# Sums of exponentials inverted in eight pieces per head inside attention, and loaded broadcast in the last projection

## The chip, the cores and the metric

The kernel runs on one NeuronCore of one Trainium2 chip. The metric is device time in microseconds (us), the median of several executions. An engine is one of TensorE (PE; its weight loads are shown as PEld), VectorE (DVE), ScalarE (ACT), GpSimd (POOL) and the engine that here only issues transfers, SyncE (SP). Each runs its own list of instructions in order and waits on semaphores for the others.

## The reference

One step of a two-layer decoder trunk over a prompt of 2048 rows and 8 sample rows, model width 1024. Layer 0 mixes a gated MLP and a linear recurrence. Layer 1 is an attention with a forget gate, 16 heads of 64 columns:

```
s = q @ k * scale + cq - ck            # cumulative log-forget bias, causal mask
p = softmax(s);  att = p @ v
y = x + (att * silu(g)) @ w_out1       # w_out1 is 1024 x 1024
```

The kernel doesn't divide by the sum of the exponentials inside the attention. It computes `exp(s - max) @ v`, gates it with silu(g), and stores it unnormalised to DRAM as `att` (1024 x 2056), beside the sums `lsum` (16 heads x 2056 columns; the 8 sample columns hold 1.0, since those rows are normalised at once). The last stage divides.

## The kernel before

The stages run one after another with a barrier between them: norm and layer 0, output projection 0, projection 1 together with the sample rows' scores, `past` (decay of the cached rows), `attention` (lines 1708 to 2260) and `out1` (2263 to 2431).

**attention.** A unit u is one head h = u // 4 and one quarter c = u % 4 of the prompt (512 query columns). It has 4(c+1) steps, one per block of 128 keys, so a head has 40 steps and the whole stage N = 640. `schedule()` (1741) writes out one list, SEQ, which every engine walks in the same order, doing its part of each entry. The entries:

- QK (step n): PE multiplies keys by queries into one of two PSUM buffers, ACT takes the exponential (2165), POOL adds it into the unit's `acc` (2037).
- M: the maximum pass, 22 steps ahead of QK. PE multiplies into MX, a ring of two PSUM buffers (2072), DVE reduces each to a maximum (2200). `ring_free` (2048) makes PE wait, before it writes a ring buffer, until the content two entries earlier has been read. There is one M at nearly every step, behind that step's QK. PE walks its list in order, so a late maximum also holds up every QK and PV behind it.
- PV: values by exponentials, for four steps at a time (2113). OE and OF finish a unit: ACT copies, DVE adds the halves (2214, 2215) and gates (2218), SP stores.
- LS (once per head): PE sums `acc` over its partitions into a ring buffer (2121), ACT copies it to `lt` (2177), SP stores one row of each 32 to `lsum` (1918). `lt` is [128, 512]: four quarters of the head, each replicated over 32 partitions.
- SD ... VC: the sample rows' attention, one batch row per 80 steps, so its small steps SD to SR fall on steps 1 to 10 of every second head only.

If E is the first step of a new head, the old head's last PV comes at E+1, its OF at E+5 and its LS at E+6. Below, "M9" stands for the maximum entry at step E+9. A boundary is called odd where E = 40, 120, ..., 600 (8 of them) and even where E = 80, 160, ..., 560 (7 of them); the sample rows' small steps are beside the even ones. The sixteenth LS stands at the very end of the list.

**out1.** 17 tiles, 16 of 128 rows and one of 8. Per tile: SP loads `att` (512 KB, 1024 pieces of 512 B) three tiles ahead (2291) and `x` (2295); DVE inverts 128 columns of the sums (2358); PE spreads the 16 inverted rows over 128 partitions with a 0/1 matrix `expand`, `turn_out` (2403 to 2410: 8 fp32 matmuls, 16 as the trace counts them); DVE multiplies (2365); ACT and DVE split the result into a high and a low part (2341, 2372); PE does `product` (2412), 48 matmuls of 512 columns recorded at lines 112 to 114; DVE adds x (2378); SP stores. `turn_out` of tile n+1 stands ahead of `product` of tile n. At the start of the stage 16 weight loads of 256 KB, ACT's high parts (2351) and DVE's low parts (2392) run beside the first product.

Of the kernel before, what the change touches and what calls it, by code (L numbers as in the profile page):

```python
# [33 lines left out]
P = 128  # L34
# [1673 lines left out]
def attention(nc, z, a, C, D, out):  # L1708
# [27 lines left out]

    def first_odd(u):

        return 0 if u % NC else P

    def schedule():
# [50 lines left out]
        for u in range(U):  # L1792
            for kb in range(blocks(u)):
                seq += loads.pop(n, [])
                for v in turn_at.pop(n, []):
                    turn(v)
                for w in later.pop(n, []):
                    if w[0] == "LS":
                        sums(w[1])
                    else:  # L1800
                        seq.append(w)
                seq.append(("QK", u, kb, n))
                for _ in range(min(2, min(len(todo), n + 1 + LEAD) - done)):
                    v = maximum()
                    if v is not None:
                        turn_at.setdefault(n + 3, []).append(v)
                if kb % G == G - 1:
                    pending.append((u, kb - G + 1, n - G + 1))
                if pending and pending[0][2] + G - 1 <= n - 2:
                    p = pending.pop(0)  # L1810
                    weigh(p)
                    if p[1] == blocks(p[0]) - G:
                        later.setdefault(n + 4, []).append(("OF", p[0]))
                        if p[0] % NC == NC - 1:
                            later.setdefault(n + 5, []).append(("LS", p[0] // NC))
                seq += side.pop(n, [])
                n += 1
# [5 lines left out]
        sums(H - 1)  # L1823
        assert n == N and done == len(todo) and not turn_at and not loads and not side
# [5 lines left out]
    with ExitStack() as ctx:  # L1830
# [53 lines left out]
        lst = S.sem("sums_stored")  # L1884
# [4 lines left out]
        def _(sp):  # L1889
# [26 lines left out]
            def store_sums(h):  # L1916
                sp.wait_ge(lsd, h + 1)
# [38 lines left out]
            for w in SEQ:  # L1956
# [4 lines left out]
                elif w[0] in ("OF", "LS"):  # L1961
                    due.append([2, *w])
# [7 lines left out]
                elif w[0] == "QK":  # L1970
                    for d in due:
                        d[0] -= 1
                    while due and due[0][0] <= 0:
                        d = due.pop(0)
                        if d[1] == "LS":
# [5 lines left out]
            for d in due:  # L1981
                if d[1] == "LS":
# [205 lines left out]
        def _(dve):  # L2188
# [6 lines left out]
            for w in SEQ:  # L2195
# [11 lines left out]
                elif w[0] == "OF":  # L2207
# [10 lines left out]
                    nc.vector.tensor_tensor(og[u % 2][:], og[u % 2][:], SG[u % 2][:], ALU.mult).then_inc(oadd, 1)  # L2218
                elif w[0] == "SD":
# [43 lines left out]
def out1(nc, z, a, C, D, out):  # L2263


    TILES = [(n, P, n * P) for n in range(z.NT)] + [(z.NT, z.B, z.T)]
    N = len(TILES)
    HALF = z.D // 512
    with ExitStack() as ctx:
# [7 lines left out]
        ls, rl = S.sb("ls", [z.H, z.TS]), S.sb("rl", [z.H, z.TS])  # L2277
        expand = S.sb("expand", [z.H, z.D])
        pp = S.ps("pp", [P, 2, z.D])
        rb = S.ps("rb", [P, 2, z.KB, P])  # L2280
        (l_in, w_hi, w_lo, exd, recd, spread, divided, m_hi, m_lo, prd, added) = S.sems(
            "lsum_in weight_hi weight_lo expanded lsum_inverted spread divided mixed_hi mixed_lo product added")
# [5 lines left out]
        def _(sp):  # L2288
            def load_mixed(n, rows, col):
                if n >= 3:  # L2290
                    sp.wait_ge(divided, n - 2)
                sp.dma_start(mt[:, n % 3, :, 0:rows],
                             D.att[:, ds(col, rows)].rearrange("(k p) t -> p k t", p=P)).then_inc(m_in[n % 3], 16)

# [10 lines left out]
            sp.dma_start(ls[:], D.lsum).then_inc(l_in, 16)  # L2305
# [18 lines left out]

        @block.gpsimd
        def _(pool):
            nc.gpsimd.memset(expand[:], 1.0).then_inc(exd, 1)
            pool.wait_ge(exd, 1)
            nc.gpsimd.affine_select(out=expand[:], in_=expand[:], compare_op=ALU.is_ge, fill=0.0, base=0,
                                    pattern=[[1, z.D]], channel_multiplier=-z.HD).then_inc(exd, 1)  # L2330
            pool.wait_ge(exd, 2)
            nc.gpsimd.affine_select(out=expand[:], in_=expand[:], compare_op=ALU.is_ge, fill=0.0, base=z.HD - 1,
                                    pattern=[[-1, z.D]], channel_multiplier=z.HD).then_inc(exd, 1)
# [22 lines left out]
        def _(dve):  # L2356
            def invert(n, rows, col):
                nc.vector.reciprocal(rl[:, ds(col, rows)], ls[:, ds(col, rows)]).then_inc(recd, 1)  # L2358

            def divide(n, rows):  # L2360
                dve.wait_ge(spread, n + 1)
# [3 lines left out]
                nc.vector.tensor_tensor(md[:, n % 2, :, 0:rows], mt[:, n % 3, :, 0:rows], rb[:, n % 2, :, 0:rows],  # L2365
# [14 lines left out]
            dve.wait_ge(l_in, 16)  # L2380
            invert(*TILES[0])
            invert(*TILES[1])
# [10 lines left out]
            for n, rows, col in TILES:  # L2393
                if n + 2 < N:
                    invert(*TILES[n + 2])
# [6 lines left out]
        def _(pe):  # L2402
            def turn_out(n, rows, col):
                pe.wait_ge(recd, n + 1)
                if n >= 2:
                    pe.wait_ge(divided, n - 1)
                for k in range(z.KB):
                    last = nc.tensor.matmul(rb[:, n % 2, k, 0:rows], expand[:, k * P:(k + 1) * P], rl[:, ds(col, rows)],  # L2408
                                            start=True, stop=True)
                last.then_inc(spread, 1)  # L2410

# [13 lines left out]

            pe.wait_ge(exd, 3)
            turn_out(*TILES[0])
            for n, rows, col in TILES:
                if n + 1 < N:
                    turn_out(*TILES[n + 1])  # L2430
                product(n, rows)
# [92 lines left out]
```

## Time and profile before

| what | us |
|---|---|
| median of 3 runs | 3041.19 (3039.72 to 3047.91) |
| the profiled execution's own time | 3042.56 |
| its span, first to last instruction | 3040.8 |
| attention, about | 1798 to 2797 of the span |
| out1, about | 2802 to 3041 of the span |
| the chain that ended last, by line (the page) | the product's lines 112, 113 and 114 2% of the span each, the spread's line 2408 1%, all others 0% |
| PE / DVE / ACT / POOL busy, share of the span | 92% / 52% / 34% / 45% |

Start times are counted in us from the first instruction. In a timeline row the first number is the start, the second how long the group lasted, and "x" how many instructions it holds; a group in square brackets is idle time of the engine before it and what ended it. The granted clock is 1.00 at TensorE's full 2.4 GHz and 0.50 at 1.2 GHz. An instruction's recorded duration runs from its start to its end; consecutive ones overlap a little, so four reductions of 0.69 us take 2.54 us together.

### The profile page before, as it was taken

How to read it: one execution, taken by the hardware profiler on the slowest of the kernel's cores; microseconds unless marked ns; L12 is line 12 of the kernel's file. 1: busy time of each engine (PE TensorE's matmuls, PEld its weight loads, DVE VectorE, ACT ScalarE, POOL GpSimd, SP SyncE). 2: the span in 40 equal slices, each digit the busy share in tenths (PEclk: the TensorE clock that was granted, in tenths of full speed). 3: DMA queues.
4: the chain of work that ended last, by engine and by line, in shares of the span. 5: the costliest groups of instructions: out<-in, count | busy, mean ns of one | idle time of the engine just before them, and what ended most of it. 6: DMA issues, size and time to landing. Idle time of an engine off the chain costs nothing. (4 is left out here: it accounts for less than half of the span.)

```text
span 3040.8 us, 46331 instructions
## 1 busy us (share of the span) xinstructions
PE 2789.8 (92%) x17133; PEld 2224.5 (73%) x17133; DVE 1592.0 (52%) x2154; ACT 1026.1 (34%) x1725; POOL 1377.5 (45%) x986
## 2 busy tenths in 40 slices
PE   3899999869989999999999739999999999998999
PEld 3899999757749989999899725555555555554887
DVE  4244333343545789865555465555645555453432
ACT  4333325312452222221122104454444455444100
POOL 0000000010003885469999836777776777776000
PEclk9999999979999999999999959999999999999999
DMA  4101111055635888788888767787897877874531
GB/s 122 44 28 47 46 35 37 14 182 173 183 119 170 293 288 276 252 276 272 268 261 275 220 152 221 207 242 217 218 252 205 240 211 221 238 212 140 168 119 63
DMA packets 327914, 547.68 MB, mean 180 GB/s; under 512 B 76093, under 2 KB 220129, under 8 KB 319212
## 3 DMA queue, kind: packets, MB, share of 16 engines
q1 hardware_dynamic: 246604, 454.31, 50.7%
q10 hardware_dynamic: 78080, 75.65, 7.6%
q0 software_dynamic: 3008, 14.81, 1.3%
q8 instruction: 135, 2.21, 0.3%
q14 instruction: 87, 0.71, 0.1%
HBM read 449.58 MB, written 95.12 MB: 179 GB/s over the span
## 5 line engine op out<-in xcount | busy, mean ns | idle before, releaser
L1174 POOL TENSOR_TENSOR p_kq<-p_kq 128x1024 f32<-128x1024 f32 x256 | 624.4, 2465 | 373.9 <-DMA p_kq<-in_cache_k_dram 373.5
L2037 POOL TENSOR_TENSOR at_acc<-at_acc,at_w 128x512 f32<-128x512 f32 (+3 forms) x576 | 645.2, 1120 | 229.5 <-ACT at_w L2165 165.7
L112 PE MATMUL p_pb<-p_w,x_xh 128*128 128x256 f32 x2048 | 593.0, 290 | 15.6 <-DVE p_w L1505 15.6
L2200 DVE TENSOR_REDUCE at_mx<-at_mx 128x1 f32<-128x512 f32 (+3 forms) x640 | 382.7, 608 | 427.2 <-PE at_mx L2072 311.9
L113 PE MATMUL p_pb<-p_w,x_xh 128*128 128x256 f32 x2048 | 580.3, 283 | 0.0
L114 PE MATMUL p_pb<-p_w,x_xl 128*128 128x256 f32 x2048 | 579.9, 283 | 0.0
L2165 ACT ACTIVATE at_w<-at_st,c_nckt 128x512 f32<-128x512 f32 (+3 forms) x640 | 389.6, 623 | 366.1 <-PE at_st L2098 193.2
L1607 DVE TENSOR_REDUCE p_sc<-p_kq 128x16 f32<-128x1024 f32 x256 | 310.0, 1216 | 201.6 <-POOL p_kq L1174 201.4
L112 PEld LDWEIGHTS p_pb<-p_w,x_xh 128*128 128x128 f32 x2048 | 391.2, 191 | 28.2 <-DVE p_w L1505 17.4
L113 PEld LDWEIGHTS p_pb<-p_w,x_xh 128*128 128x128 f32 x2048 | 392.9, 192 | 0.0
L114 PEld LDWEIGHTS p_pb<-p_w,x_xl 128*128 128x128 f32 x2048 | 392.1, 191 | 0.0
L112 PE MATMUL l_pb<-x_xh,l_wh 128*128 128x412 f32 x800 | 290.8, 364 | 7.4 <-DVE l_wl L875 7.4
L2113 PE MATMUL at_o<-at_w,at_v 128*64 128x512 f32 (+3 forms) x1280 | 282.7, 542 | 0.5 <-ACT at_w L2165 0.5
L114 PE MATMUL l_pb<-x_xh,l_wl 128*128 128x412 f32 x800 | 280.4, 350 | 0.0
L113 PE MATMUL l_pb<-x_xl,l_wh 128*128 128x412 f32 x800 | 280.2, 350 | 0.0
L2072 PE MATMUL at_mx<-at_km,at_q 128*128 128x512 f32 (+3 forms) x640 | 250.2, 393 | 28.8 <-POOL at_onesh L2012 21.6
L2096 PE MATMUL at_st<-at_q,at_k 128*128 128x512 f32 (+3 forms) x640 | 263.9, 412 | 0.8 <-ACT at_w L2165 0.8
L112 PE MATMUL o_pp<-o_wh,o_mh 128*128 128x512 f32 (+1 forms) x544 | 221.3, 407 | 35.1 <-DVE o_wl L586 22.2
L2098 PE MATMUL at_st<-at_q,at_k 128*128 128x512 f32 (+3 forms) x640 | 235.2, 367 | 0.0
L2096 PEld LDWEIGHTS at_st<-at_q,at_k 128*128 128x128 f32 x640 | 121.2, 189 | 135.9 <-issue 111.2
L113 PE MATMUL o_pp<-o_wl,o_mh 128*128 128x512 f32 (+1 forms) x544 | 216.7, 398 | 0.0
L114 PE MATMUL o_pp<-o_wh,o_ml 128*128 128x512 f32 (+1 forms) x544 | 216.2, 397 | 0.0
(296 smaller groups left out, 3802.9 us busy)
## 6 DMA issues: line engine op xcount, KB each, us to landing
p_kq<-in_cache_k_dram SPq DMA_DIRECT2D x256, 512.0 KB, 4.7
at_vp<-in_cache_v_dram SPq DMA_DIRECT2D x256, 512.0 KB, 5.2
o_mt<-mixed SPq DMA_DIRECT2D x32, 512.0 KB, 4.9
p_raw<-in_w_in_dram ACTq DMA_DIRECT2D x32, 512.0 KB, 5.8
at_q<-qh SPq DMA_DIRECT2D x32, 512.0 KB, 10.5
at_k<-kh SPq DMA_DIRECT2D x32, 512.0 KB, 8.2
l_raw<-in_w_in_dram SPq DMA_DIRECT2D x20, 512.0 KB
mixed<-l_w POOLq DMA_DIRECT2D x8, 1028.0 KB, 4.2
```

Of the source, the lines that this page charges most:

```text
L112: nc.tensor.matmul(out, lhs[0], rhs[0], start=(k == 0), stop=False)
L113: nc.tensor.matmul(out, lhs[0], rhs[1], start=False, stop=False)
L114: return nc.tensor.matmul(out, lhs[1], rhs[0], start=False, stop=(k == nk - 1))
L1174: nc.gpsimd.tensor_tensor(kq[:, slot[page]], kq[:, slot[page]], kq[:, slot[query]], ALU.mult).then_inc(kmul, 1)
L1607: nc.vector.tensor_reduce(sc[:, b % 2].rearrange("p (h g) -> p h g", g=z.PG)[:, :, r], by_head(kq[:, slot["p", g]], z.H), AX.X, ALU.add).t ...
L2037: nc.gpsimd.tensor_tensor(t[:, 512 - wd:512], t[:, 512 - wd:512], W[n % RW][:, 0:wd], ALU.add).then_inc(accd, 1)
L2072: last = nc.tensor.matmul(MX[r % 2][:, 0:wd], Q2[s][:, t * P:(t + 1) * P], KM[s][:, seg * 512:seg * 512 + wd], start=True, stop=seg < c)
L2096: nc.tensor.matmul(ST[n % 2][:, 0:wd], K1[s][:, ks], Q1[s][:, q0:q0 + wd], start=True, stop=False)
L2098: last = nc.tensor.matmul(ST[n % 2][:, 0:wd], K2[s][:, ks], Q2[s][:, q0:q0 + wd], start=False, stop=not diagonal)
L2113: last = nc.tensor.matmul(O[u % 2][y:y + HD, 512 - wd:512], V[s][:, kb + x, :], W[(n + x) % RW][:, 0:wd], start=kb + x < 2, stop=kb + x >= ...
L2165: nc.scalar.activation(W[n % RW][:, 0:wd], ST[n % 2][:, 0:wd], ACT.Exp, bias=C.nckt[:, kb, u // NC:u // NC + 1]).then_inc(ex, 1)
L2200: nc.vector.reduce_max(mx[:, u % 2, j, seg:seg + 1], MX[r % 2][:, 0:wd], AX.X).then_inc(mread, 1)
```

## The change

Two parts that need each other. In attention, DVE inverts `lt` in place before it is stored, in DC = 8 pieces of 64 columns per head, one at the head of each of the steps E+7 to E+14 (an entry "OI"); the last head's eight pieces stand at the end of the list. Piece 0 waits for ACT's copy of the sums. SP's store of the head's row waits for the eighth piece. `lsum` in DRAM then holds inverted sums.

In out1, the load of the sums, DVE's inversions, POOL's build of `expand` and all of PE's `turn_out` go. In their place SP issues, directly behind each load of an `att` tile, two DMAs that read the tile's 8 even and 8 odd head rows from DRAM and write each to 64 partitions, into `rb` in SBUF (three buffers). DVE's multiply waits for them instead of for PE, and reads both inputs from SBUF.

```
+    DC = 8
...
                         if p[0] % NC == NC - 1:
                             later.setdefault(n + 5, []).append(("LS", p[0] // NC))
+                            for x in range(DC):
+                                later.setdefault(n + 6 + x, []).append(("OI", x, p[0] // NC))
...
         sums(H - 1)
+        for x in range(DC):
+            seq.append(("OI", x, H - 1))
...
             def store_sums(h):
-                sp.wait_ge(lsd, h + 1)
+                sp.wait_ge(linv, DC * (h + 1))
...
-                elif w[0] in ("OF", "LS"):
-                    due.append([2, *w])
+                elif w[0] == "OF" or w[0] == "OI" and w[1] == DC - 1:
+                    due.append([2, w[0], w[-1]])
...
+                elif w[0] == "OI":
+                    _, x, h = w
+                    cols = slice(512 // DC * x, 512 // DC * (x + 1))
+                    if x == 0:
+                        dve.wait_ge(lsd, h + 1)
+                    nc.vector.reciprocal(lt[:, cols], lt[:, cols]).then_inc(linv, 1)
...
+                for x in range(2):
+                    sp.dma_start(rb[x * z.HD:(x + 1) * z.HD, n % 3, :, 0:rows],
+                                 D.lsum[:, ds(col, rows)].rearrange("(k x) t -> x k t", x=2)[x].partition_broadcast(z.HD)).then_inc(r_in[n % 3], 16)
...
-            sp.dma_start(ls[:], D.lsum).then_inc(l_in, 16)
...
-                dve.wait_ge(spread, n + 1)
+                dve.wait_ge(r_in[n % 3], 32 * (n // 3 + 1))
...
-                nc.vector.tensor_tensor(md[:, n % 2, :, 0:rows], mt[:, n % 3, :, 0:rows], rb[:, n % 2, :, 0:rows],
+                nc.vector.tensor_tensor(md[:, n % 2, :, 0:rows], mt[:, n % 3, :, 0:rows], rb[:, n % 3, :, 0:rows],
...
-                for k in range(z.KB):
-                    last = nc.tensor.matmul(rb[:, n % 2, k, 0:rows], expand[:, k * P:(k + 1) * P], rl[:, ds(col, rows)],
-                                            start=True, stop=True)
...
-            pe.wait_ge(exd, 3)
-            turn_out(*TILES[0])
             for n, rows, col in TILES:
-                if n + 1 < N:
-                    turn_out(*TILES[n + 1])
                 product(n, rows)
```

## Rows read from the trace of the kernel before

**Rows 1.** The chain that ended last, in order of time, in out1: start, us, what.

```profile
2801.76 3.21 DMA o_ls<-lsum
...
2806.08 3.76 PE o_rb L2408 x16
...
2867.25 1.98 PE o_rb L2408 x16
...
2880.33 1.98 PE o_rb L2408 x16
```

**Rows 2.** Windows: length; busy (count) of PE, PEld, DVE, ACT, POOL; clock, DMA share, GB/s.

```profile
1798.00:2797.00 999.00, 966.54 (x5320) 553.87 (x5320) 537.33 (x947) 482.04 (x793) 717.63 (x664) 0.99 0.78 218
1951.13:1958.00 6.87, 5.75 (x31) 3.55 (x29) 6.76 (x14) 3.25 (x6) 5.35 (x6) 1.00 0.51 115
2806.00:2814.60 8.60, 7.16 (x32) 6.90 (x32) 5.04 (x7) 4.73 (x8) 0.00 (x0) 0.50 1.07 364
2814.60:2819.40 4.80, 4.79 (x11) 3.81 (x12) 4.80 (x9) 3.61 (x8) 0.00 (x0) 0.50 1.05 390
2869.00:2882.10 13.10, 13.10 (x67) 10.81 (x65) 4.45 (x5) 1.06 (x1) 0.00 (x0) 1.00 0.39 121
3013.97:3017.38 3.41, 3.41 (x10) 2.67 (x9) 0.00 (x0) 0.00 (x0) 0.00 (x0) 0.50 0.17 67
```

**Rows 3.** Timeline of PE at the start of one tile of out1.

```profile
2866.86 0.39 PE L114 MATMUL o_pp<-o_wh,o_ml 128*128 128x512 f32 x1
2867.18 2.05 PE L2408 MATMUL o_rb<-o_rl,o_expand 16*128 16x128 f32 x16
2869.16 0.50 PE L112 MATMUL o_pp<-o_wh,o_mh 128*128 128x512 f32 x1
```

**Rows 4.** Groups by line and shape, DVE's reciprocals: busy us, mean ns, idle before.

```profile
L2358 DVE RECIPROCAL o_rl<-o_ls 16x128 f32<-16x128 f32 x16 | 14.8, 930 | 7.9 <-DMA o_ls<-lsum 7.9
...
L903 DVE RECIPROCAL l_ss<-l_ss 128x16 f32<-128x16 f32 x4 | 1.0, 254 | 21.5 <-ACT l_ss L839 21.5
```

**Rows 5.** Timeline at the first odd boundary (E = 40): ACT, DVE and PE.

```profile
1888.41 0.60 ACT L2177 ACTIVATE at_lt<-at_mx 128x512 f32<-128x512 f32 x1 [2.24 <-PE at_mx L2121]
...
1889.27 1.39 DVE L2200 TENSOR_REDUCE at_mx<-at_mx 128x1 f32<-128x512 f32 x2 [3.47 <-PE at_mx L2072]
...
1890.89 0.69 DVE L2200 TENSOR_REDUCE at_mx<-at_mx 128x1 f32<-128x512 f32 x1 [0.23 <-PE at_mx L2072]
...
1892.98 0.41 DVE L2200 TENSOR_REDUCE at_mx<-at_mx 128x1 f32<-128x256 f32 x1
...
1894.17 2.54 DVE L2200 TENSOR_REDUCE at_mx<-at_mx 128x1 f32<-128x512 f32 x4 [0.78 <-PE at_mx L2072]
...
1895.01 0.40 PE L2072 MATMUL at_mx<-at_km,at_q 128*128 128x512 f32 x1
...
1895.71 0.34 PE L2072 MATMUL at_mx<-at_km,at_q 128*128 128x384 f32 x1
...
1900.33 2.20 DVE L2200 TENSOR_REDUCE at_mx<-at_mx 128x1 f32<-128x512 f32 x3 [3.63 <-PE at_mx L2072]
```

**Rows 6.** Timeline at the first even boundary (E = 80): DVE and PE.

```profile
1951.13 1.28 DVE L2200 TENSOR_REDUCE at_mx<-at_mx 128x1 f32<-128x512 f32 x2
...
1957.38 1.83 DVE L2200 TENSOR_REDUCE at_mx<-at_mx 128x1 f32<-128x512 f32 x3
...
1958.15 0.40 PE L2072 MATMUL at_mx<-at_km,at_q 128*128 128x384 f32 x1
```

**Rows 7.** Timeline at the end of attention: DVE and SP.

```profile
2796.24 0.68 DVE L2218 TENSOR_TENSOR at_og<-at_og,at_sg 64x512 f32<-64x512 f32 x1
...
2797.51 0.52 SPq L1918 DMA_DIRECT2D lsum<-at_lt  x1
```

**Rows 8.** DMA issues: out<-in, engine, count, KB each, median us to landing.

```profile
o_mt<-att SPq DMA_DIRECT2D x16, 512.0 KB, 4.8
...
o_gb<-in_norm_g_dram SPq DMA_DIRECT2D x1, 512.0 KB, 8.3
```

More of the change, by code:

```diff
@@ L1883, in attention @@
         ogst = S.sems("out_stored0 out_stored1")
-        lst = S.sem("sums_stored")
+        lst, linv = S.sem("sums_stored"), S.sem("sums_inverted")
         v_in = S.sems("pages_in0 pages_in1")
@@ L1974, in _ @@
                         d = due.pop(0)
-                        if d[1] == "LS":
+                        if d[1] == "OI":
                             store_sums(d[2])
@@ L1981, in _ @@
             for d in due:
-                if d[1] == "LS":
+                if d[1] == "OI":
                     store_sums(d[2])
@@ L2276, in out1 @@
         xt = S.sb("x", [P, 3, z.D])
-        ls, rl = S.sb("ls", [z.H, z.TS]), S.sb("rl", [z.H, z.TS])
-        expand = S.sb("expand", [z.H, z.D])
+        rb = S.sb("rb", [P, 3, z.KB, P])
         pp = S.ps("pp", [P, 2, z.D])
-        rb = S.ps("rb", [P, 2, z.KB, P])
-        (l_in, w_hi, w_lo, exd, recd, spread, divided, m_hi, m_lo, prd, added) = S.sems(
-            "lsum_in weight_hi weight_lo expanded lsum_inverted spread divided mixed_hi mixed_lo product added")
+        (w_hi, w_lo, divided, m_hi, m_lo, prd, added) = S.sems(
+            "weight_hi weight_lo divided mixed_hi mixed_lo product added")
+        r_in = S.sems("rsum_in0 rsum_in1 rsum_in2")
         w_in = [S.sem(f"weight_in{m}") for m in range(HALF * z.KB)]
@@ L2323, in _ @@
                 sp.wait_ge(y_st[s], 16 * len(range(s, N, 3)))
[L2325 to L2333, printed above, removed]
         @block.scalar
@@ L2356, in _ @@
         def _(dve):
-            def invert(n, rows, col):
-                nc.vector.reciprocal(rl[:, ds(col, rows)], ls[:, ds(col, rows)]).then_inc(recd, 1)
             def divide(n, rows):
-                dve.wait_ge(spread, n + 1)
+                dve.wait_ge(r_in[n % 3], 32 * (n // 3 + 1))
                 dve.wait_ge(m_in[n % 3], 16 * (n // 3 + 1))
@@ L2378, in add @@
                 nc.vector.tensor_tensor(xt[0:rows, n % 3, :], xt[0:rows, n % 3, :], pp[0:rows, n % 2, :], ALU.add).then_inc(added, 1)
-            dve.wait_ge(l_in, 16)
-            invert(*TILES[0])
-            invert(*TILES[1])
             divide(0, P)
@@ L2393, in _ @@
             for n, rows, col in TILES:
-                if n + 2 < N:
-                    invert(*TILES[n + 2])
                 if n + 1 < N:
@@ L2402, in _ @@
         def _(pe):
[L2403 to L2406, printed above, removed]
-                for k in range(z.KB):
-                    last = nc.tensor.matmul(rb[:, n % 2, k, 0:rows], expand[:, k * P:(k + 1) * P], rl[:, ds(col, rows)],
-                                            start=True, stop=True)
-                last.then_inc(spread, 1)
             def product(n, rows):
```

## The prediction

> **What bounds the kernel now.** I read the chain that ended last by line (in the table above), the same chain in order of time, the windows, and then timelines around the places that the diff touches. The chain is PE throughout out1: the product's three lines with 2% each, and the spreading of the sums (line 2408) with 1%. That 1% is on the path, not beside it: in order of time [rows 1] a spread of 16 matmuls takes 1.98 us in every tile, and the tiles repeat every 13.08 us (2880.33 less the same point of the tile before, 2867.25). The window of one tile [rows 2] shows PE busy for all 13.10 us, DVE for 4.45, ACT for 1.06 and the DMA engines for 0.39 of the time. So PE alone sets out1. Attention too is PE's: busy 966.5 of 999 us, DVE 537 [rows 2]. But DVE's 54% is a mean: at the heads' boundaries of the even kind it is busy 6.76 of 6.87 us. The change moves work from PE in out1 to DVE in attention, exactly to these boundaries, so two sums have to be made and set against each other.
>
> **Out1: what goes from PE.** In a steady tile the spread takes 1.98 us [rows 1]. The product's last matmul before it lasts 0.32 us to the next start (2867.18 less 2866.86) where one otherwise follows after 0.23, and I take the same 0.09 behind it [rows 3]. That is 2.16 us per tile, 15 times (the spreads of tiles 2 to 16; those of tiles 0 and 1 stand ahead of the first product): 32.4 us. Nothing else is near: DVE's three passes over a tile, with or without the inversion of 0.93 us [rows 4], are under 5 us of a tile that will take 10.9.
>
> The clock: the window 3013.97 to 3017.38 is at 0.50, right behind the last tile's spread, whose matmuls have only 8 columns [rows 2]. It costs half of 3.41 us, 1.7 us, and with the spread gone the product runs without that pause. I take 1.7; the bounds are 0 and 1.7. Out1: 34.1 us.
>
> **Out1: its start.** Today the load of the sums takes 3.21 us, the inversion and the cold spread of two tiles follow, and the first multiply starts behind 3.76 us of spreading from 2806.08, 8.1 us into the stage; the product starts at 2814.60 [rows 1, 2]. In the new order the multiply waits for two broadcast DMAs that are issued directly behind the `att` tile. Such a tile lands 4.8 us after its issue [rows 8]; with two more issues ahead that is some 5.7 us into the stage, 2.4 us earlier. But ACT's high part of the tile stands behind two weight conversions, and the weights now stand behind 512 KB more in SP's queue, 1.3 us at the 390 GB/s of that stretch [rows 2]. I take a gain of 1.0 us; the bounds are +2.4 and -1.0.
> Two costs I take at nothing, with their covers. First, the weights of the second half stand behind 1 MB more, 2.7 us. What covers it is that the first 11 matmuls are cold and take 4.8 us for less than four blocks of weights, while DVE, busy through those 4.8 us, makes about seven [rows 2]. Without that cover it costs up to 2.7 us. Second, the clock. PE worked on the spreads for 7.16 of the 8.6 us from 2806 and stayed at 0.50; it rose only after 4.8 us of the dense product [rows 2]. So I take the spreads to have warmed nothing, and 11 cold matmuls again. If they did count, the product would be cold for the 13.3 us that lay between the first spread and the rise, 8.5 us more at half speed: 4.3 us lost.
>
> **Out1: the broadcast loads.** Each tile gets 512 KB more in 1024 pieces of 512 B, the shape of the `att` tile, which lands in 4.8 us [rows 8]. The trace has one broadcast of this size, the norm's gain over 128 partitions: 8.3 us to landing, behind other loads [rows 8]. By the window the DMA engines are busy 0.39 of 13.1 us with 1.5 MB [rows 2]. The new load adds a third of that (1.7 us) if it costs as the others; to bind it would have to add more than 5.8 us (10.9 less 5.1). It is issued three tiles ahead, so its latency is covered. I take 0; the uncovered end is the rival below.
>
> **Attention: one piece.** The trace has no reciprocal of 128x64. Between 16 columns (254 ns) and 128 columns (930 ns) the slope is 6.04 ns per column [rows 4], which makes 64 columns 544 ns. Instructions in sequence overlap: four reductions of 690 ns take 2.54 us [rows 5], 0.62 us each from start to start and 0.07 less than their duration. So a piece takes 0.48 us of DVE. Eight per head and 16 heads are 61 us. The bounds are 0.42 (its share of 128 columns, less the overlap) and 0.54 (no overlap).
> The Trainium skill ("VectorE: DVE Perf Modes", section "Walkthrough: the 8-slice pipeline in each mode") has the reciprocal as an iterative division with a repeat count of 8, on an engine that the same page puts at 0.96 GHz. By that rule 64 columns would take an estimated 533 ns without any fixed part, some 0.60 us from start to start, and the loss below would grow by about a quarter, the time to some 3043. The rows' 6.04 ns per column contradict it, and the trace has the vote.
>
> **Attention: an odd boundary [rows 5].** ACT's copy ends at 1889.01, before DVE is ready, so piece 0 waits for nothing. Today M6 and M7 are read from 1889.27, M8 from 1890.89, OF is 1.48 us, M9 starts at 1892.98, and M10 to M13 from 1894.17. The pieces enter at the head of their steps: M6 89.27, piece 0 89.89, M7 90.37, piece 1, M8 91.47, piece 2, OF 92.57, M9 94.05 (ends 94.46), piece 3, M10 94.87, piece 4, M11 95.97, ends 96.66. The ring passes it on: PE's M13 waits for the read of M11, plus 0.15 us from a read's end to PE's start (M10 ends at 94.86, M12 starts at 95.01). So M13 starts at 96.8 where it started at 1895.71: 1.1 us late. Behind M13 PE has a PV and a page of values, in which DVE catches up (today its last read ends at 1896.71 and the next starts at 1900.33, after 3.63 us of idling), so pieces 6 and 7 cost nothing. Nothing returns the 1.1 us, since what follows on PE in its list just shifts. 8 boundaries: 8.8 us.
>
> **An even boundary [rows 2, 6].** M7 is read from 1951.13 and M11 from 1957.38, and in between DVE hardly idles, since the sample rows' small steps stand there. Ahead of M11 come five pieces, 0 to 4, each in full: M11 is read 2.4 us later, from 1959.78, and ends at 1960.47. M13 then starts at 1960.6 where it started at 1958.15: 2.45 us late. 7 boundaries: 17.2 us. Odd and even together 26.0 us. The bounds: 0, if PE's lateness is taken back by waits that it would have had anyway; and 57.6, if all of the 15 x 8 x 0.48 us shows.
>
> **The end of attention [rows 7].** Here nothing covers the pieces. DVE's last gating ends at 2796.92; the eight pieces follow and end at 2796.9 + 7 x 0.48 + 0.54 = 2800.8. SP's store of the last sums moves from 2797.51 to 2800.85, and the two stores and the barrier behind it move as much: 3.3 us.
> SP's queue at the other boundaries: the store of the sums moves from behind step E+8 to behind E+16 and waits for the eighth piece, which by then is done; the loads ahead of it only come earlier. ACT's next copy into `lt` is 32 steps away. I take 0.
>
> **The sum.** -32.4 - 1.7 - 1.0 + 8.8 + 17.2 + 3.3 = -5.8 us. The profiled execution took 3042.56, of which the span is 3040.8; it comes to 3036.8. The median is 1.4 lower, so I expect 3035.4.
>
> **The rivals.**
> (a) *The pieces hide.* PE is at 97% in attention but DVE idles for 460 us; if the lateness of M only eats into waits that PE has there anyway (33 us in the stage), the odd boundaries or all of them cost nothing. For it: PE idles that much. Against: M12 and M13 start 0.70 us apart [rows 5], which is three matmuls of 0.23 us and no gap. With the odd ones free 3026.6; with all free 3009.4.
> (b) *The head boundary becomes DVE's (slower).* Place: the steps E+7 to E+14, whose maxima are late. Price: up to 57.6 us. It decides from 2.1 us per boundary on average (-35.1 + 3.3 + 15x is 0 there; 2.7 for slower by 0.3%), against the 1.73 that I work out. Half of the pieces' full time shown, 28.8 us, would give 3038.2; all of it, 3067.0; some 45 us, 3054. For it: the even boundaries have no slack, and a late M13 pushes ACT and POOL, which I left out. Against: DVE's idle stretch behind M13.
> (c) *The broadcast binds out1, or the clock.* 64 partitions read the same rows. If a load took as long as the 8.3 us that the norm's broadcast took from issue to landing [rows 8], a tile would need 13.4 us and the gain of 32.4 would turn to a loss of some 5: 3073. With only the longer cold start, 3039.7.
> (d) *It doesn't do what it says*: the product slows where the spread was, for instance by cold stretches. It gives half of 32.4 back: 3051.6. Nothing in the rows speaks for it.
>
> **How the numbers follow.** A run of this kernel is told from no change at about 0.3%, 9.1 us. Forecast 0.52, with its own range 3025 to 3045; (a) 0.24; (b) 0.15; (c) 0.06; (d) 0.03. The forecast lies inside 0.3%, and a fifth of it falls beyond on the fast side. Faster: 0.10 + 0.22 = 0.32. Slower: 0.12 of (b), 0.04 of (c), 0.02 of (d), 0.18. Same: 0.50. The range 3020 to 3054 leaves out the far ends of (a) and (b).
>
> **What would show it.** Out1's tiles repeat every 10.9 us with PE dense, no half-speed stretch near the last tile, the multiply never waiting for `rb`. Reciprocals of 128x64 near 0.54 us. At an odd boundary M13 starts 1.1 us later against the head's first QK, at an even one 2.4, so two heads take about 3.6 us more than today. The stage out1 starts 3.3 us later against the last PV. The prediction is wrong if the two heads' period grows by under 1 or over 6 us, or if a tile of out1 takes over 11.2 us.

## The result, and the profile after

The changed kernel takes 3099.64 us (median of 4 runs, 3096.95 to 3105.33) beside 3044.13 for the kernel before on the same chip (4 runs; the 3041.19 of the table above is the median of the first three): a ratio of 1.0188, 95% interval 1.0168 to 1.0207. It is slower by 1.9%. The prediction was 3035.4 us with a range of 3020 to 3054, so it was wrong, and the place of the loss, the broadcast loads, stood only in its rival (c). The profiled execution has a span of 3096.8 us at a mean granted clock of 0.962.

The chain that ended last, by engine and by line, on the page of the changed kernel. Before, it was PE with the product's three lines and the spread.

```profile
DMA 5%; SPq 2%; PE 1%; DVE 1%; ACT 0%; issue 0%; DVEq 0%
DMA o_mt<-att 3%; DMA o_rb<-lsum 1%; SPq L2307 1%; DMA o_raw<-in_w_out_dram 0%; SPq L2324 0%; PE o_pp L112 0%; PE o_pp L113 0%; PE o_pp L114 0%; SPq L2318 0%; SPq L2304 0%; DVE o_x L2379 0%; DVE o_wl L2390 0%; DVE o_md L2366 0%; SPq L2313 0%; DVE o_ml L2373 0%
```

The last stage isn't PE's any more. Its loads and the queue that issues them set the end: in order of time the chain runs through a store of the output, the issue of the next `att` load, its landing and DVE's addition. Windows of the same kernel: 180 us in the middle of out1, and one tile of it (columns as in [rows 2]):

```profile
2880.00:3060.00 180.00, 149.18 (x596) 118.49 (x595) 45.82 (x39) 13.75 (x13) 0.00 (x0) 0.93 0.51 141
2905.65:2920.51 14.86, 11.78 (x45) 9.26 (x44) 3.58 (x4) 1.06 (x1) 0.00 (x0) 0.89 0.46 128
```

One tile before was 13.10 us with PE busy for all of it [rows 2]. Now it is 14.86 us with PE busy for 11.78. PE does less work per tile, as the change meant it to, but it waits for 3.1 us of it, and part of its work runs at the lower clock (0.89 over the tile). DVE's timeline shows for what (start, duration, what; in brackets the idle time ahead and what ended it):

```profile
2905.65 1.23 DVE L2366 TENSOR_TENSOR o_md<-o_mt,o_rb 128x1024 f32<-128x1024 f32 x1 [9.55 <-DMA o_rb<-lsum]
2907.99 1.23 DVE L2373 TENSOR_TENSOR o_ml<-o_md,o_mh 128x1024 fp32r<-128x1024 f32 x1 [1.12 <-ACT o_mh L2345]
2909.14 1.21 DVE L2379 TENSOR_TENSOR o_x<-o_x,o_pp 128x1024 f32<-128x1024 f32 x1
2920.51 1.22 DVE L2366 TENSOR_TENSOR o_md<-o_mt,o_rb 128x1024 f32<-128x1024 f32 x1 [10.16 <-DMA o_rb<-lsum]
```

Each multiply waits some 10 us for its broadcast. The view of the tile `rb` sums that up: its loads (SP) with the minimum, median and maximum of their issue in ns, who waited, and the time from issue to landing.

```profile
L2307 SPq DMA_DIRECT2D o_rb<-lsum x34: 617/2825/5131, 2827.3 to 3064.4; - x34
...
  DMA o_rb<-lsum: 158.2, 16
...
DMA to landing us min/median/max: 9.0/14.9/19.3
```

A load takes a median of 14.9 us to land, where the `att` tile of before, with the same 1024 pieces of 512 B in 512 KB, took 4.8 [rows 8]; each `rb` load moves only half of that. Its issue holds SP for a median of 2.8 us, and all other loads of the stage stand in the same queue. DVE waited 16 times, 158.2 us in all. The other loads are slowed with it. The DMA view of 2880 to 2990 us has (KB each, median us to landing):

```profile
o_mt<-att SPq DMA_DIRECT2D x8, 512.0 KB, 13.2
o_rb<-lsum SPq DMA_DIRECT2D x15, 256.0 KB, 15.4
o_x<-x SPq DMA_DIRECT2D x7, 512.0 KB, 13.0
```

Before, an `att` tile landed in 4.8 us [rows 8]. The DMA engines were busy for only 0.51 of the stretch from 2880 to 3060: this slowness is no lack of engines' time, and the busy share doesn't show it.

Attention went nearly as worked out. Reciprocals of the new shape (busy us, mean ns), then ACT's copies of a head's sums, first and last start, of the kernel before and of the changed one:

```profile
L2230 DVE RECIPROCAL at_lt<-at_lt 128x64 f32<-128x64 f32 x128 | 67.5, 531 | 0.0
```
```profile
L2177 ACT ACTIVATE at_lt<-at_mx x16: 597/598/598, 1888.4 to 2796.0; 128x512 f32<-128x512 f32 x16
```
```profile
L2183 ACT ACTIVATE at_lt<-at_mx x16: 597/597/598, 1885.8 to 2818.3; 128x512 f32<-128x512 f32 x16
```

From the first to the last copy, over 15 boundaries, it was 907.6 us and is 932.5: 24.9 us lost. Behind the last copy the store of the sums is issued 4.36 us later (2822.66) where it was 1.51 [rows 7]: 2.85 us. The two make 27.75. Out1 took 239.0 us from its first load (2801.76, [rows 1]) to the end, and takes 269.9 (2826.88 to 3096.8): 30.9 us lost, where 35.1 were to be gained. The stages ahead of attention ended 2.6 us earlier, which the change can't have caused. The sum, 27.75 + 30.9 - 2.6, is the 56 us between the two spans.

### The profile page after: what moved, and what is told of

It is laid out like the page before. It is cut to its first block and busy times, and to the rows that moved or that the text cites. A ratio compares the mean times of both kernels' runs of the same rounds, so it can differ in the third digit from the quotient of the medians.

```text
span 3096.8 us, 45912 instructions
## 1 busy us (share of the span) xinstructions
PE 2772.2 (90%) x16861; PEld 2193.1 (71%) x16861; DVE 1631.0 (53%) x2265; ACT 1027.0 (33%) x1725; POOL 1378.3 (45%) x983
```

## The experiments

All times are medians in us, ratios are to the kernel before in runs on the same chip. The groups of experiments ran on different chips, where the kernel before took 3039.95 to 3045.43, so a difference of a few us between two groups says little. "The changed kernel" is the subject of this document; the parts of it are varied one by one.

### Which half costs what

**Attention's part alone**: the pieces at the heads' boundaries as changed, out1 as before, with a copy in place of its inversion:

```diff
-                nc.vector.reciprocal(rl[:, ds(col, rows)], ls[:, ds(col, rows)]).then_inc(recd, 1)
+                nc.vector.tensor_copy(rl[:, ds(col, rows)], ls[:, ds(col, rows)]).then_inc(recd, 1)
```

> Only attention's part of the change: the eight reciprocals per head stay, out1 is the one of before, with a copy in place of its own inversion. By my working, and by the trace after the change (the sixteenth sums' store comes 27.7 us later, counted from the first head's LS, than before), this costs 26 to 29 us against before: 3070 to 3073. If out1's new loads or the earlier end of attention had a part in attention's loss, it would be less. The theory that attention carries the whole loss of 56 us gives 3100.

Measured 3071.08, ratio 1.0091 (1.0064 to 1.0118): 28.3 us over the 3042.74 of before, and 13.08 us per tile in out1. Attention's loss stands by itself and adds up with the other half.

**Broadcast loads for three tiles only**:

```diff
-                for x in range(2):
+                for x in range(2 if n < 3 else 0):
...
-                dve.wait_ge(r_in[n % 3], 32 * (n // 3 + 1))
+                if n < 3:
+                    dve.wait_ge(r_in[n % 3], 32)
```

> The changed kernel, but only the first three tiles of out1 load the broadcast sums; the later tiles multiply by what the buffers hold, so their results are not the reference's. If the broadcast loads are what makes out1 slow, its tiles repeat every 10.9 us, out1 takes some 204 us in place of 270, and the time is 3035 to 3041: the blind forecast's own figure. The rival, that out1 is slow for another reason (the clock, the multiply with both inputs in SBUF, the missing spread), gives 3090 to 3100.

Measured 3054.08, ratio 1.0034 (1.0024 to 1.0044). From the fifth multiply on they start every 10.88 us, as I had forecast for all. But the start stays slow: the six loads that are left land after a median of 14.4 us. The expectation, 3035 to 3041, missed their cost of 13 us and more. So the loads are slow even where they are few.

### Why the broadcast loads are slow

**Distinct rows**: loads of the same shape and number, from 64 different rows of `att` in place of one row of the sums for 64 partitions:

```diff
-  D.lsum[:, ds(col, rows)].rearrange("(k x) t -> x k t", x=2)[x].partition_broadcast(z.HD)
+  D.att[:, ds(col, rows)].rearrange("(k x d) t -> x d k t", x=2, d=z.HD)[x]
```

> The changed kernel, with the same two loads per tile (64 partitions, 8 runs of 512 B each) from as many different rows of att in place of 8 rows read by all 64 partitions; the values are not the sums, so the results are not the reference's. Theory 1, reading the same DRAM bytes 64 times is what is slow: the loads hide, 3037 to 3045. Theory 2, loads that fill only 64 partitions are slow, and theory 3, 1024 more runs of 512 B per tile are too many: it stays at 3090 to 3100.

Measured 3040.12, ratio 0.9996 (0.9982 to 1.0011): 59 us faster than the changed kernel, with as many bytes into the same buffers. The landing takes a median of 6.6 us. Neither the size, the 512 B pieces, the number of SP's issues nor the writes to SBUF are the cause; it lies in what is read. I took it to be that the partitions read the same bytes. But the edit changes a second thing: the eight pieces of a partition now lie 128 rows of `att` apart, about 1 MB, in place of two rows of the sums. The next experiments take the two apart.

**One load for all 128 partitions**, from eight rows:

```diff
+  sp.dma_start(rb[:, n % 3, :, 0:rows], D.lsum[0:z.KB, ds(col, rows)].partition_broadcast(P))
...
```

> The changed kernel, with one broadcast load per tile over all 128 partitions (8 runs of 512 B each, the same bytes and the same number of runs, 8 source rows in place of 16); half of the partitions get the other head's sums, so the results are not the reference's. Theory 1 (same bytes read many times): as slow as the change or slower, 3095 to 3130. Theory 2 (half of the partitions): 3037 to 3050. Theory 3 (number of runs): 3090 to 3100.

Measured 3110.25, ratio 1.0220 (1.0192 to 1.0247). Twice the readers of half the rows is a little slower still.

**Runs of 4 KB**: the sums are stored tile by tile, so that what one partition reads is one stretch; the readers are still 64:

```diff
+  sp.dma_start(D.rsum[0:z.NT, h % 2, h // 2, :].rearrange("(c j) n -> c j n", j=4),
+               lt[0:P:32, :].rearrange("c (j n) -> c j n", j=4)).then_inc(lst, 16)
...
+  D.rsum[n, x, :, 0:rows].partition_broadcast(z.HD)
...
-    D.lsum = dram("lsum", (z.H, z.TS))
+    D.rsum = dram("rsum", (z.NT + 1, 2, z.KB, P))
```

> The changed kernel, with the inverted sums stored so that each of the 64 partitions of a broadcast load reads one run of 4 KB: 128 runs of 4 KB per tile in place of 1024 of 512 B. The bytes are the same, each still read by 64 partitions. If what makes the loads slow is that many partitions read the same bytes, however they are cut (theory 1a), the tiles of out1 still repeat every 12 to 15 us and the time stays at 3090 to 3110. If it is the number of short reads of the same rows (theory 1b), the loads land like the others, the tiles repeat every 10.9 us and the time is 3037 to 3045.

Measured 3039.96, ratio 0.9984 (0.9974 to 0.9994). The same bytes read 64 times aren't slow in themselves: theory 1a (many readers, however the bytes are cut) fell. Theory 1b, many short reads of the same rows, was left.

**Copies in DRAM**: the 32 equal rows of a head's sums, which stand in SBUF anyway, are all stored, and each is read by two partitions, in four loads of 128 KB per tile (32 partitions each) in place of two of 256 KB:

```diff
-  sp.dma_start(D.lsum[h:h + 1, 0:T].rearrange("o (c n) -> (o c) n", n=512), lt[0:P:32, :])
+  sp.dma_start(D.lrep[h].rearrange("c r n -> (c r) n"), lt[:])
...
+  src = (D.lrep.rearrange("(k x) c r n -> x c r k n", x=2)[x, c, :, :, P * j:P * j + P] if rows == P
...
```

> The changed kernel, with all 32 copies of a head's inverted sums that stand in SBUF stored to DRAM (256 KB per head in place of 8 KB), so that out1 loads 32 distinct rows twice: each byte in DRAM is read by 2 partitions in place of 64. The computation is the reference's. By theory 1 (the same bytes read many times) the tiles repeat every 10.9 us and the time is that of the kernel with distinct rows, 3037 to 3043, the store at the end of attention being up to 2 us longer. If repeated reading hurts even twice, or the 256 KB stores slow attention, over 3045.

Measured 3041.43, ratio 0.9978 (0.9966 to 0.999). In the profile the median landing is 5.2 us, for loads half as large. Here the eight pieces of a partition lie 524,288 B apart, and with two readers each that does no harm.

**Short reads again, but near to each other**: as the runs of 4 KB, with the eight pieces 1 KB apart, so that a tile again takes 1024 reads of 512 B.

```diff
-    D.rsum = dram("rsum", (z.NT + 1, 2, z.KB, P))
+    D.rsum = dram("rsum", (z.NT + 1, 2, z.KB, 2 * P))
```

> The kernel whose partitions read one run of 4 KB (3039.96 us), with the eight pieces of 512 B of a run set 1 KB apart in DRAM in place of adjoining: again 1024 reads of 512 B per tile and 64 partitions for each, as in the changed kernel, but within 8 KB in place of 8 rows 16.6 KB apart. If short reads of the same bytes are the cause (theory 1b), the tiles repeat every 12 to 15 us again and the time is 3090 to 3110. If it is that the rows lie 16.6 KB apart (theory 1c), it stays at 3037 to 3043.

Measured 3038.64, ratio 0.9995 (0.9985 to 1.0005). Theory 1b fell too: 64 readers of short pieces are fast when these lie close. What was left is where the pieces lie: their distance (1c), its not being a multiple of 512 B (1d), or that neighbouring tiles read from the same rows (1e). A mistake of mine has to be told here: the expectations of this experiment and of the one with 16,640 B apart take the changed kernel's pieces to lie 16.6 KB (16,640 B) apart. Its rows hold 2048 + 8 floats, 8224 B, and the pieces of one partition are two rows, 16,448 B, apart: only 64 B more than 16,384.

**Four distances**, each the last number of the same line (4160, 4096, 1024 and 160 floats):

> As the kernel with the pieces 1 KB apart (3038.64 us), with the eight pieces 16,640 B apart, as the rows of the changed kernel are; each tile still has an area of its own. If the distance makes the broadcast slow (theory 1c), or its not being a multiple of 512 B (theory 1d), the tiles repeat every 12 to 15 us: 3085 to 3110. If it is that neighbouring tiles read from the same rows of DRAM (theory 1e), 3037 to 3043.

> The pieces 16,384 B apart, a multiple of 512 B. Theory 1c (distance): slow, 3085 to 3110 or more. Theory 1d (alignment) and 1e: 3037 to 3043.

> The pieces 4096 B apart. Theory 1c gives something between 3038 and 3110, by how the distance counts; slow in full if the pieces must only lie in different stretches of 4 KB. Theories 1d and 1e: 3037 to 3043.

> The pieces 640 B apart, close but not on multiples of 512 B, as the rows of the changed kernel. Theory 1d (alignment): slow, 3085 to 3110. Theories 1c and 1e: 3037 to 3043.

**The changed kernel with longer rows**, and the distance of the changed kernel in separate areas (4112 floats):

```diff
-    D.lsum = dram("lsum", (z.H, z.TS))
+    D.lsum = dram("lsum", (z.H, 2080))
```

> The changed kernel with one number changed: the rows of the sums in DRAM are 2080 floats long in place of 2056, so the eight pieces that a partition reads lie 16,640 B apart in place of 16,448. The computation is the reference's. If the distance, close to 16,384 B, makes the broadcast slow (theory 1f), the time is that of the layout with separate areas at 16,640 B: 3038 to 3048. If what matters is that neighbouring tiles read from the same rows (theory 1e), 3085 to 3105.

> The changed kernel with rows of 2304 floats: pieces 18,432 B apart, 2048 more than 16,384. Theory 1f: 3037 to 3048. Theory 1e: 3085 to 3105.

> Separate areas for the tiles, pieces 16,448 B apart, the distance of the changed kernel. Theory 1f with closeness counting: 3070 to 3100. If only the exact multiple (16,384) is slow, 3039 to 3048, and the changed kernel's slowness needs the shared rows beside it.

What was measured, beside the changed kernel and the two others with 64 readers (landing of the `rb` loads from each profile):

| pieces of a partition apart, B | layout | landing, median us | time, us | ratio (95%) |
|---|---|---|---|---|
| 16,448 | rows of the changed kernel | 14.9 | 3099.64 | 1.0188 (1.0168 to 1.0207) |
| 16,384 | area per tile | 14.1 | 3078.30 | 1.0128 (1.0086 to 1.0169) |
| 16,448 | area per tile | 11.5 | 3050.72 | 1.0030 (1.0013 to 1.0047) |
| 4096 | area per tile | 9.7 | 3048.08 | 1.0015 (1.0004 to 1.0027) |
| 16,640 | area per tile | 6.7 | 3043.43 | 1.0004 (0.9991 to 1.0018) |
| 16,640 | rows of 2080 floats | 7.3 | 3044.80 | 1.0001 (0.9989 to 1.0012) |
| 18,432 | rows of 2304 floats | 6.6 | 3038.12 | 0.9983 (0.9969 to 0.9997) |
| 1024 | area per tile | 6.7 | 3038.64 | 0.9995 (0.9985 to 1.0005) |
| 640 | area per tile | 6.8 | 3039.01 | 0.9983 (0.9970 to 0.9996) |
| 512 (one run) | area per tile | 6.3 | 3039.96 | 0.9984 (0.9974 to 0.9994) |

Alignment (theory 1d) falls with 640 B. The sharing of rows between tiles (1e) falls as sole cause twice: separate areas are slow at 16,384 B, and shared rows are fast at 16,640 and 18,432. Distance as such (1c) falls too, since 16,640 and 18,432 B are fast. What is left is theory 1f, a distance at or close to 16,384 B, with a smaller loss at 4096. Several of the forecasts missed in size: 16,384 B cost less than its 3085 to 3110, and 16,448 B in separate areas (3050.72) lies in neither of its two ranges, so closeness counts, but for far less than in the changed kernel. At 16,640 B a little is left: in both kernels the first product starts 14.1 and 14.4 us behind the stage's first load, where it is 12.5 to 12.7 with 18,432, 1024 and 640 B. The view of `rb` with 16,384 B apart, then with rows of 2080 floats, shows the two ends:

```profile
L2309 SPq DMA_DIRECT2D o_rb<-rsum x34: 617/2260/4773, 2826.7 to 3040.6; - x34
...
  DMA o_rb<-rsum: 132.5, 16
...
DMA to landing us min/median/max: 7.3/14.1/16.6
```
```profile
L2307 SPq DMA_DIRECT2D o_rb<-lsum x34: 594/1051/4984, 2832.8 to 2998.7; - x34
...
  DMA o_rb<-lsum: 17.3, 2
...
DMA to landing us min/median/max: 3.6/7.3/11.8
```

With 24 floats more per row, and nothing else changed, DVE waits at the start (twice) and then never again, and 55 us are gone. The DMA view of 2880 to 2990 us has the same contrast in its queue row (packets, MB, share of 16 engines' time), first for the changed kernel, then with rows of 2080:

```profile
q1 hardware_dynamic: 17277, 15.02, 49.6%
```
```profile
q1 hardware_dynamic: 24922, 22.14, 75.4%
```

A packet occupied an engine for about as long in both (0.496 x 16 x 110 us / 17277 = 51 ns, and 53 ns), so the lost time lies between packets, not in them. Not every slower landing costs time: at 4096 B apart a load lands in 9.7 us, and from the fourth tile on the multiplies still start every 10.88 us; only the start is slower.

### Why the pieces cost, and whether they must

**One late reciprocal**: attention's part alone, with one reciprocal of 128x512, listed where the eighth piece was, seven steps behind the first, where DVE idles [rows 5]:

```diff
-    DC = 8
+    DC = 1
-   later.setdefault(n + 6 + x, []).append(("OI", x, p[0] // NC))
+   later.setdefault(n + 13 + x, []).append(("OI", x, p[0] // NC))
```

> Attention's part alone (out1 spreads by products as before, but copies the sums in place of inverting them), with the eight pieces made one reciprocal of 128x512 that stands behind the reads of step E+14, where DVE idles for 3.63 us at an odd boundary [rows 5]. Eight pieces at steps E+7 to E+14 cost 28.3 us. By the theory that they cost because they stand ahead of reads that PE waits for, one reciprocal of some 3.2 us costs at the boundaries 0 to 0.5 us each, and 3.3 at the end: 3046 to 3054. If DVE's total work sets a boundary, wherever it stands, the cost stays at 20 us and over: 3064 to 3072.

Measured 3045.40, ratio 0.9999 (0.9988 to 1.0009). Its copies run from 1883.2 to 2791.7, 908.5 us: 15 boundaries cost 0.9 us together in place of 24.9. The time is a little under the 3046 to 3054 of the expectation.

**Eight pieces, all at step E+14**:

```diff
-   later.setdefault(n + 6 + x, []).append(("OI", x, p[0] // NC))
+   later.setdefault(n + 13, []).append(("OI", x, p[0] // NC))
```

> Attention's part alone with the eight pieces of 128x64, all at step E+14 in place of E+7 to E+14 (out1 spreads by products and copies the sums). The work of DVE is that of the kernel that cost 28.3 us. If the place alone makes the cost, it goes with the one late reciprocal: 3045 to 3050, the eight being 0.6 us longer in all. If the number of pieces matters beside the place, over 3054.

Measured 3042.76 beside 3039.95, ratio 1.0009 (0.9996 to 1.0021), first and last copy 907.6 us apart as in the kernel before. DVE does the same work in the same eight pieces, and no boundary loses anything. The place is the whole cost at the boundaries; the cutting was of no use.

### Both repairs

**Copies in DRAM and one late reciprocal**, then **runs of 4 KB and one late reciprocal** (the edits are those above):

> Both repairs together: the 32 copies in DRAM, read twice each, and one reciprocal of 128x512 behind the reads of step E+14. The computation is the reference's. Out1 gains some 32 us as with distinct rows, attention loses what one late reciprocal costs (3 to 10 us): 3014 to 3024, ratio 0.990 to 0.994. If the late reciprocal costs as much as eight pieces, 3037 to 3043.

> Runs of 4 KB for the broadcast loads, and one reciprocal of 128x512 at step E+14. The computation is the reference's. The same two gains as with the 32 copies (3013.47 us), without the 256 KB stores: 3009 to 3016, ratio 0.988 to 0.990. If the copies' version gained by something else, 3018 and over.

Measured 3013.47 with a ratio of 0.9887 (0.987 to 0.9903), and 3011.28 with 0.9901 (0.9884 to 0.9918). Both are about 1% faster than the kernel before and nearly 3% faster than the changed one. The second one's profile is what the change was to look like. At the first odd boundary the inversion stands in DVE's idle stretch, and the next read is still waiting for PE:

```profile
1892.56 2.53 DVE L2208 TENSOR_REDUCE at_mx<-at_mx 128x1 f32<-128x512 f32 x4 [0.78 <-PE at_mx L2080]
1895.01 3.34 DVE L2232 RECIPROCAL at_lt<-at_lt 128x512 f32<-128x512 f32 x1
1898.72 2.20 DVE L2208 TENSOR_REDUCE at_mx<-at_mx 128x1 f32<-128x512 f32 x3 [0.37 <-PE at_mx L2080]
```

In out1 DVE's multiply never waits in the steady part, and windows show PE dense, with the last tile at full clock:

```profile
2854.51 1.22 DVE L2368 TENSOR_TENSOR o_md<-o_mt,o_rb 128x1024 f32<-128x1024 f32 x1
...
2865.39 1.22 DVE L2368 TENSOR_TENSOR o_md<-o_mt,o_rb 128x1024 f32<-128x1024 f32 x1
```
```profile
2816.00:2821.00 5.00, 4.51 (x11) 3.54 (x12) 3.45 (x6) 1.25 (x3) 0.00 (x0) 0.50 1.08 260
2821.00:2826.00 5.00, 5.00 (x22) 4.12 (x21) 3.71 (x6) 4.10 (x7) 0.00 (x0) 0.94 1.06 392
2850.00:2990.00 140.00, 140.00 (x619) 115.95 (x618) 44.56 (x39) 12.98 (x13) 0.00 (x0) 1.00 0.63 172
2965.00:2999.00 34.00, 34.00 (x152) 26.16 (x151) 7.61 (x8) 1.93 (x3) 0.00 (x0) 1.00 0.22 72
```

## Why the prediction was wrong, step by step

**The step that failed: "Out1: the broadcast loads ... I take 0".** That sum took the load at 1.7 us of DMA time on the ground that it has the shape of the `att` tile, asked whether 5.8 us of engines' time were free, and took the latency as covered. The engines' time was free: they are half idle in the changed kernel too. (The load is dearer than 1.7 us even when it is fast: with rows of 2080 floats the engines are busy for 0.754 of a tile of 10.88 us, 8.2 us, 3.1 more than the 5.1 before.) What the term left out is that landing time can grow from another cause than the engines' load. The two loads of a tile were put at 0 and cost 59 us of the whole (3099.64 against 3040.12 with distinct rows, 3039.96 with one run and 3044.80 with longer rows, at an unchanged attention).

The cover of "three tiles ahead" is smaller than it sounds. With fast loads the `att` load of a tile is issued 21.3 us ahead of its multiply (2844.12 to 2865.39 in the kernel with both repairs and 4 KB runs), two tiles. In the changed kernel the tile whose multiply starts at 2920.51 has its `att` load issued at 2896.82, but the two `rb` loads hold the queue for 5.95 us from 2899.81. The second is issued at 2904.91, which leaves 15.6 us, just what it takes to land.

```profile
2896.82 2.95 SPq L2304 DMA_DIRECT2D o_mt<-att  x1
```

**Rival (c) had the place right, and the length of its tile by luck.** From the 8.3 us to landing of the norm's broadcast [rows 8] it came to a tile of 13.4 us (8.3 and the 5.1 of the other loads), at a chance of 0.06. The tiles came to 12.2 to 15.4 us, but not in that way: at 4096 B apart the loads landed in 9.7 us and no steady tile was longer than 10.88. Together with attention's loss the time went beyond even its 3073, which had only the forecast's attention in it and no slow start. Before the first product there were 12.85 us from the stage's first load (2801.76 to 2814.61); with slow broadcasts it is 21.5 (2826.88 to 2848.34). The first multiply waits for its broadcast until 2843.08, 16.2 us into the stage where it was 8.1, and the first weights, which stand behind the broadcasts in the queue, are there no earlier (ACT converts them from 2843.65).

**Out1, what goes from PE (34.1 us): right, but hidden.** With fast loads the tiles repeat every 10.88 us (2865.39 less 2854.51), against 13.08 [rows 1], 2.20 per tile where 2.16 was worked out. Near the last tile the window from 2965 to 2999 is at 1.00, so the half-speed stretch of [rows 2] is gone with the spread of 8 columns. The other kernels bear that out: in the four profiles that still spread (the kernel before and the three with attention's part alone) some eight matmuls of the last product run at half speed behind the last spread, in the ten that I read without it none does. Out1 takes 205.4 us in the kernel with both repairs and 4 KB runs (2804.39 to 3009.8), 33.6 less than before; the prediction has 35.1. Most of the difference is a wait of 1.24 us ahead of the second tile's product, which the sum put at nothing.

**The start (1.0): of the right sign, too large. The clock (0): right.** In the same kernel the first product stands at 2816.49, 12.1 us behind the first load in place of 12.85: 0.75 us gained. In seven others with landings under 7 us it is 0.2 to 0.4 us. The window up to 2821 is at 0.50 with 11 matmuls, the number of before [rows 2], and the next at 0.94. That the numbers are equal is luck: the matmuls of the first product that run slower than the rest number 8 to 13 in the four profiles with spreads ahead of them and 7 to 14 in fourteen without. But there is no sign that the spreads had warmed anything: PE spread for 7.16 us at 0.50 before, and the 8.5 us more at half speed that the alternative asks for are in no profile.

**One piece (544 ns, 0.48): right in duration, a little high in effect.** It takes 531 ns. Alternating with the reads, a read and a piece take 1.00 us from start to start of the next read, where a read alone takes 0.62 [rows 5]: a net 0.38 per piece, for 0.48 in the prediction. Timeline of DVE in the changed kernel, first odd boundary, and PE's M13 there:

```profile
1886.71 0.69 DVE L2206 TENSOR_REDUCE at_mx<-at_mx 128x1 f32<-128x512 f32 x1 [3.46 <-PE at_mx L2078]
1887.32 0.54 DVE L2230 RECIPROCAL at_lt<-at_lt 128x64 f32<-128x64 f32 x1
1887.78 0.63 DVE L2206 TENSOR_REDUCE at_mx<-at_mx 128x1 f32<-128x512 f32 x1
1888.32 0.54 DVE L2230 RECIPROCAL at_lt<-at_lt 128x64 f32<-128x64 f32 x1
1888.78 0.63 DVE L2206 TENSOR_REDUCE at_mx<-at_mx 128x1 f32<-128x512 f32 x1
```
```profile
1894.32 0.44 PE L2078 MATMUL at_mx<-at_km,at_q 128*128 128x384 f32 x1
```

**The odd boundary (1.1): right.** From the read of M6 to PE's M13 it was 1895.71 - 1889.27 = 6.44 us [rows 5] and is 1894.32 - 1886.71 = 7.61: 1.17 later, by the ring as described.

**The even boundary (2.45): right in kind, too large at the first.** From the read ahead of piece 0 (a sample's scores) to PE's M13 it was 7.63 us (1950.52 to 1958.15, the end in [rows 6]) and is 9.28 (below): 1.65. Five pieces at the net 0.38 make 1.9.

```profile
1949.21 0.70 DVE L2249 TENSOR_TENSOR at_sd<-at_sd,at_cv 128x528 f32<-128x528 f32 x1
```
```profile
1958.49 0.44 PE L2078 MATMUL at_mx<-at_km,at_q 128*128 128x384 f32 x1 [0.29 <-DVE at_mx L2206]
```

The starts of ACT's copies, one per head, give every boundary: the interval to the next copy grew by 1.22 to 1.27 us at seven of the eight odd ones and by 2.8 at the last. At the seven even ones it grew by 0.9 to 2.5, 1.9 on average, and three of them by 2.4 to 2.5 as forecast. Over all 15 boundaries 24.9 us were lost where 26.0 were forecast: the total is nearer than its parts, as the odd ones cost more than 8.8 (11.5) and the even ones less than 17.2 (13.3). Every boundary cost something, the least 0.9 us, so rival (a) fell, and with the total rival (b)'s 57.6 too.

**The end of attention (3.3): 2.85.** The eight last pieces, as DVE and SP have them in the changed kernel:

```profile
2819.21 3.42 DVE L2230 RECIPROCAL at_lt<-at_lt 128x64 f32<-128x64 f32 x8
```
```profile
2822.66 0.51 SPq L1924 DMA_DIRECT2D lsum<-at_lt  x1
```

**The Trainium skill's rule on the reciprocal.** With 531 ns for 64 columns the estimate by the Trainium skill ("VectorE: DVE Perf Modes", section "Walkthrough: the 8-slice pipeline in each mode") seems met by its 533. But eight in sequence take 3.42 us, 0.41 from start to start, where the prediction made 0.60 of the rule. A single duration can't tell the rule from the rows' slope. The late one has 512 columns and takes 3342 ns, so (3342 - 531) / 448 = 6.27 ns per column, near the 6.04 of [rows 4]; by the rule 512 columns would be an estimated 4267 ns. The measurement decides against it.

The kernel with both repairs (4 KB runs) bears out the rest of the sum: out1 33.6 less, attention 4.1 more (913.2 us from the first copy to the store of the sums, 2799.99, against 909.1), 29.5 us less by these parts and 28.7 between the medians, 3011.28 and 3039.95.

## What to carry to other kernels

When a load is new, its shape and bytes aren't enough to price it: write down which addresses the partitions read at one time. Where many read the same ones, lay the source out as one run per partition or pad its rows, a change of one number that was worth 55 us here. If the only broadcast in the trace lands late, price that case in full rather than as a mishap, and count the cover from the issue in the queue, not in buffers. A piece of work for an engine with a ring around it goes behind the last read that the other engine waits for, whole; cut small and spread over the tight steps, each piece ahead of such a read costs its time.

## What the runs showed of the hardware

A broadcast from DRAM to 64 partitions is slow where the eight pieces that each partition reads lie 16,384 B apart (14.1 us to landing) or nearly (14.9 at 16,448 in the changed kernel's rows, 11.5 in separate areas), less so at 4096 B (9.7), and not at 16,640 or 18,432 B (6.6 to 7.3) or within 8 KB (6.3 to 6.8). Many readers alone are not enough, as the fast rows show. Whether a distance alone is enough isn't shown: no run has pieces 16,384 B apart with few readers, and the nearest, 524,288 B apart (a multiple of 16,384) with two readers, landed in 5.2 us in loads of half the size. The DMA engines' busy share falls meanwhile, to 0.50 (changed kernel) from 0.75 (rows of 2080 floats).

The Trainium skill ("DMA: Bandwidth & Descriptors", section "Latency and other measured facts") has a rule of this kind: copies whose partitions' rows lie at large powers of two apart, 2 MiB and more, lose bandwidth, and a pad of a few KiB restores it while 192 B don't. I had not weighed it, as it speaks of distinct rows at a far larger pitch. The runs agree in kind and differ in both numbers: here 16,384 B is enough when 64 partitions read the same bytes, and 256 B beyond it restore the speed but for some 1.5 us at the stage's start, 64 B in part.

Left open is why the changed kernel's own layout (3099.64) is slower than separate areas at its own distance (3050.72). The two differ in that the second half's pieces lie one row of 8224 B from the first half's, near 8192, and in that the loads of up to three tiles in flight read from the same rows. Longer rows cure both at once, so no run tells them apart. In the separate areas, too, the distance of the pieces sets how far apart the halves and the tiles lie, so "distance" stands here for the whole layout. That such addresses fall to the same part of the memory is an inference; the runs show only the distances.
